# Fourteen projection units of each layer with a 512-column moving operand, and an evacuation in two steps

## What is computed

```python
u = rmsnorm(x, norm_mix[l])
proj = u @ w_in[l]                       # 1024 -> 5444 columns
q, k, v, iq, ik, iw, cB, cC, ch, g = jnp.split(proj, offsets, axis=-1)
y_attn = dsa_attention(q, k, v, iq, ik, iw) @ w_attn_out[l]      # top-64 keys by an index score
y_conv = (cB * short_conv(cC * ch, conv_w[l])) @ w_conv_out[l]
gates = jax.nn.sigmoid(g.reshape(B, T, N_BRANCH, D))
x = x + (gates[:, :, 0] * y_attn + gates[:, :, 1] * y_conv) @ w_mix_out[l]
u = rmsnorm(x, norm_mlp[l])
x = x + jnp.square(jax.nn.relu(u @ w_mlp_up[l])) @ w_mlp_down[l]
```

## Time and profile before

| | |
|---|---|
| median of three runs | 1065.11 us (1063.73 to 1068.13) |
| the profiled execution, its own time | 1065.51 us |
| its span, first to last instruction | 1063.7 us |
| busy: TensorE matmul, weight load | 1034.1 us (97%), 893.5 us (84%) |
| busy: VectorE, ScalarE, GpSimd | 708.1 us (67%), 535.5 us (50%), 69.6 us (7%) |
| granted TensorE clock, mean | 0.997 |

### The profile page before, as it was taken

How to read it: one execution, slowest core, us unless ns; L and a number is a source line. 1 busy time by engine, 2 the same in 40 slices (tenths; PEclk the granted TensorE clock), 3 DMA queues, 4 the chain that set the end, 5 groups by cost and what they waited for, 6 DMA issues and landing times.

```text
span 1063.7 us, 16558 instructions
## 1 busy us (share of the span) xinstructions
PE 1034.1 (97%) x6205; PEld 893.5 (84%) x6205; DVE 708.1 (67%) x1073; ACT 535.5 (50%) x687; POOL 69.6 (7%) x80
## 2 busy tenths in 40 slices
PE   8989989999999999999999999999999999999997
PEld 7865778888888899998788888888999987888886
DVE  6876766666667676768665656576776676655654
ACT  7546565444456544455634444375444645534443
POOL 1000000000000308000000000012170000000000
PEclk9999999999999999999999999999999999999999
DMA  9974335555555663248465563665622675566520
GB/s 296 215 236 153 119 114 203 198 172 192 174 183 164 202 189 120 77 172 292 133 209 189 178 212 109 222 200 159 199 95 85 220 236 172 185 197 199 161 95 39
DMA packets 130654, 185.16 MB, mean 174 GB/s; under 512 B 4361, under 2 KB 106399, under 8 KB 130591
## 3 DMA queue, kind: packets, MB, share of 16 engines
q1 hardware_dynamic: 130503, 184.25, 54.4%
q10 hardware_dynamic: 88, 0.04, 0.0%
HBM read 180.91 MB, written 1.56 MB: 172 GB/s over the span
## 4 chain that ended last, share of the span: by engine, by line
PE 89%; ACT 3%; DVE 3%; DMA 1%; SPq 1%; issue 1%; ACTq 0%; DVEq 0%
PE wide L553 17%; PE acc L516 9%; PE acc L517 9%; PE acc L518 9%; PE wide L554 9%; PE wide L516 7%; PE wide L517 7%; PE wide L518 7%; PE wide L536 3%; PE wide L529 3%; PE wide L530 3%; ACT whi L967 2%; SPq L430 1%; PE acc L686 1%; DVE wlo L1261 1%
## 5 line engine op out<-in xcount | busy, mean ns | idle before, releaser
L1261 DVE TENSOR_TENSOR wlo<-raw,whi 128x2048 fp32r<-128x2048 f32 (+1 forms) x178 | 386.8, 2180 | 155.5 <-ACT whi L967 154.3
L967 ACT ACTIVATE whi<-raw 128x2048 fp32r<-128x2048 f32 (+1 forms) x178 | 322.1, 1819 | 107.7 <-PE wide L518 43.9
L553 PE MATMUL wide<-uhl,whi 128*128 128x512 f32 x864 | 307.6, 399 | 4.5 <-DVE wlo L1261 4.5
L554 PE MATMUL wide<-uhl,wlo 128*128 128x256 f32 x864 | 242.4, 281 | 0.0
L553 PEld LDWEIGHTS wide<-uhl,whi 128*128 128x128 f32 x864 | 162.3, 188 | 44.9 <-DVE wlo L1261 5.8
L554 PEld LDWEIGHTS wide<-uhl,wlo 128*128 128x128 f32 x864 | 163.2, 189 | 1.4
L516 PE MATMUL acc<-whi,mhi 128*128 128x512 f32 x376 | 147.7, 393 | 1.9 <-DVE wlo L1261 1.7
L516 PE MATMUL wide<-uhl,whi 128*128 128x256 f32 x512 | 146.9, 287 | 1.1 <-DVE wlo L1346 1.0
L517 PE MATMUL acc<-wlo,mhi 128*128 128x512 f32 x376 | 146.8, 390 | 0.0
L518 PE MATMUL acc<-whi,mlo 128*128 128x512 f32 x376 | 146.6, 390 | 0.0
L517 PE MATMUL wide<-uhl,whi 128*128 128x256 f32 x512 | 144.9, 283 | 0.0
(11 more groups left out here) (248 smaller groups left out, 1212.4 us busy)
## 6 DMA issues: line engine op xcount, KB each, us to landing
raw<-in_w_in SPq DMA_DIRECT2D x49, 1024.0 KB, 5.4
raw<-in_w_mlp_up SPq DMA_DIRECT2D x32, 1024.0 KB, 5.8
raw<-in_w_mlp_down SPq DMA_DIRECT2D x32, 1024.0 KB, 4.9
raw<-in_w_gate SPq DMA_DIRECT2D x11, 1024.0 KB, 5.5
raw<-in_w_up SPq DMA_DIRECT2D x11, 1024.0 KB, 5.5
raw<-in_w_down SPq DMA_DIRECT2D x11, 1024.0 KB, 5.6
raw<-in_w_mix_out SPq DMA_DIRECT2D x8, 1024.0 KB, 5.3
raw<-in_w_out SPq DMA_DIRECT2D x4, 1024.0 KB, 10.9
```

What stands on the lines that cost most here:

```text
L553: pe.matmul(col[2 * n + c][:], whi_v(u)[:, f, cs], uhl[:, f, :], start=start, stop=False)
L554: return pe.matmul(col[2 * n + c][:, 0:T], wlo_v(u)[:, f, cs], uhl[:, f, 0:T], start=False, stop=stop)
L967: act.activation(whi[:, u.buf, 0:size], raw[:, u.slot, 0:size], ACT.Copy).then_inc(w_hi, 1)
L1261: dve.tensor_tensor(wlo[:, u.buf, 0:size], raw[:, u.slot, 0:size], whi[:, u.buf, 0:size].bitcast(F32), ALU.subtract).then_inc(w_lo, 1)
```

## The change

The units 8 to 21 of both layers go through `wide_features(u, j % 2)`: 32 matmuls, 16 of 512 and 16 of 256 columns, into both banks of the pair `wide[j % 2]`. A unit now shares its banks with the unit two before it, so TensorE waits from j = 10 on for the evacuation of unit j-2 (before: of unit j-4). The wait for the tokens of unit 7 comes at j = 9 and no longer at j = 10. The evacuation is in three instructions: ScalarE copies the low halves into the destination (it waits for the matmuls, in iteration j, behind the split and ahead of the copy of the probabilities), then VectorE, where L1570 stood, adds the high halves from the banks, waits for its own result (`link`), and multiplies by `rnb`.

```diff
@@ TensorE, the loop over a layer's units
-                    if j >= L_FIRST:
-                        pe.wait_ge(w_lo, u.upto())
-                    if j in (4, 6, 8, 10):
-                        pe.wait_ge(evac, A_TOKENS + L_TOKENS * l + j // 2 - 1)
-                    if j >= 12:
-                        pe.wait_ge(fevac, A_FEATURES + L_FEAT * l + j - 11)
+                    if j in (4, 6, 8, 9):
+                        pe.wait_ge(evac, A_TOKENS + L_TOKENS * l + (4 if j == 9 else j // 2 - 1))
+                    if j >= 10:
+                        pe.wait_ge(fevac, A_FEATURES + L_FEAT * l + j - 9)
...
                     else:
-                        col_features(u, col[j % 4], uhi, ulo)
+                        pe.wait_ge(w_lo, u.upto())
+                        wide_features(u, j % 2)
@@ ScalarE
                     elif j in (3, 5, 7):
                         evacuate_tokens(u, j, (qtok, ktok, vtok)[j // 2 - 1])
+                    elif j >= L_FIRST:
+                        act.wait_ge(used, u.upto())
+                        if j in (8, 10):
+                            act.wait_ge(qk_ps, 4 * (1 + l) + j - 6)
+                        act.activation(feature_dst(j), wide[j % 2][:, :, T:2 * T], ACT.Copy).then_inc(flow, 1)
@@ VectorE, feature_evac(j)
-                    dve.wait_ge(used, l_unit(l, j).upto())
...
-                    if j in (8, 10):
-                        dve.wait_ge(qk_ps, 4 * (1 + l) + j - 6)
-                    dve.tensor_tensor(dst, col[j % 4][:].rearrange("p (c t) -> p c t", c=2),
-                                      rnb[:].unsqueeze(1).broadcast_to([P, 2, T]), ALU.mult).then_inc(fevac, 1)
+                    dve.wait_ge(flow, L_FEAT * l + j - L_FIRST + 1)
+                    link(dve.tensor_tensor(dst, wide[j % 2][:, :, 0:T], dst, ALU.add))
+                    dve.tensor_tensor(dst, dst, rnb[:].unsqueeze(1).broadcast_to([P, 2, T]), ALU.mult).then_inc(fevac, 1)
```

More of the change, by code:

```diff
@@ L78 @@
 G_N = G_LAYER + LAYERS * LG_N
-LAYER_LINKS = 91
+LAYER_LINKS = 105
 L_FIRST = 8
@@ L266, in build @@
         fevac = sem("fevac")
+        flow = sem("flow")
         rn_ok = sem("rn_ok")
@@ L391, in mid, with feature_dst @@
             return buf[:, 2 * s:2 * s + 2, :]
+        def feature_dst(j):
+            return (cC, cH, cB)[(j - 8) // 2][:, 2 * (j % 2):2 * (j % 2) + 2, :] if j < 14 else \
+                big[:, 2 * (j - 14):2 * (j - 14) + 2, :]
         def t_bank(a, h):
@@ L1562, in feature_evac @@
                 def feature_evac(j):
-                    dst = (cC, cH, cB)[(j - 8) // 2][:, 2 * (j % 2):2 * (j % 2) + 2, :] if j < 14 else \
-                        big[:, 2 * (j - 14):2 * (j - 14) + 2, :]
-                    dve.wait_ge(used, l_unit(l, j).upto())
+                    dst = feature_dst(j)
                     if j == L_FIRST:
                         dve.wait_ge(rb_sb, 3 + l)
-                    if j in (8, 10):
-                        dve.wait_ge(qk_ps, 4 * (1 + l) + j - 6)
-                    dve.tensor_tensor(dst, col[j % 4][:].rearrange("p (c t) -> p c t", c=2),
-                                      rnb[:].unsqueeze(1).broadcast_to([P, 2, T]), ALU.mult).then_inc(fevac, 1)
+                    dve.wait_ge(flow, L_FEAT * l + j - L_FIRST + 1)
+                    link(dve.tensor_tensor(dst, wide[j % 2][:, :, 0:T], dst, ALU.add))
+                    dve.tensor_tensor(dst, dst, rnb[:].unsqueeze(1).broadcast_to([P, 2, T]), ALU.mult).then_inc(fevac, 1)
                 dve.tensor_copy(lg[:], gcol[:, bass.ds(l * LG_N + G_LAYER, LG_N)]).then_inc(lg_ok, 1)
```

## The result

The changed kernel takes 1084.87 us (median of four runs, 1083.03 to 1086.01); the ratio to the kernel before is 1.0154, with a 95% interval of 1.0129 to 1.0179. It is slower, as forecast, but by more: the forecast was 1078.0, and the median lies 0.9 us above the range of 1072 to 1084. On the 1065.11 us from which forecast and range were worked out, the ratio gives 1081.5 us, inside the range. The runs of one kernel lie up to 9 us apart (29 runs of the kernel before in a later comparison: 1063.14 to 1071.77, median 1068.48), and the slower ones show the lower granted clock of TensorE: a mean of 0.989 to 0.993 in the six slowest of the 29, of 0.993 to 0.997 in the eight fastest. In the changed kernel's trace the clock falls well under 1 at five places during matmuls, and four of them lie outside the changed stretches.

What follows compares the result with a forecast made beforehand. TensorE, busy 97% of the span, was taken as the bound, so each new wait counts in full. Matmul savings against evacuation waits lose 6.5 us a layer, 13.0 on 1065.51, less 0.4 for the median: 1078.0 us, range 1072 to 1084.

Steps and rivals of the forecast that it cites:

- the walk: Start times computed unit by unit from unit 8 to unit 23, each waiting for the evacuation two units before.
- Term 1: TensorE's matmuls, units 8 to 21: 5.63 us a unit instead of 5.76, saving 0.13 each, 3.6 over 28 units.
- Term 2: Units 8 to 13: evacuation lag grows from 5.03 to 6.26 us, so the stage loses 1.00 us.
- Term 3: Units 14 to 19: the add lengthens VectorE's and ScalarE's softmax loop by 2.92 us; unit 19 starts 6.1 us later.
- the old meeting: One softmax step a layer beside GpSimd's long multiplication, 2.57 us against a median of 0.33; the loop grew by 1.3.
- The bound: Meetings with GpSimd may not come back, 1075.5 us, or may cost another 1 us a layer, 1080.
- GpSimd is held up: Rival, chance 0.20: the new multiplication from SBUF delays GpSimd or softmax steps, 2 us a layer more, 1082.
- Term 4: Units 20 to 23: unit 23 waits 0.5 us for unit 21's evacuation; the layer loses 6.5 us.
- The sum: Both layers: 2 x 6.5 = 13.0 us on 1065.51, with the median 0.4 lower: 1078.0 us.
- The clock rival: Rival, chance 0.06: TensorE's new waits lower its clock in both layers' stages, some 10 us more, 1088.
- It fits: Rival, chance 0.08: evacuations finish in time, TensorE keeps its stride and gains 3.6 us, 1061.5.

Runs made afterwards that it cites:

- the reordered one: Changed kernel with VectorE's evacuation (add and multiplication) of unit j-1 moved ahead of its split of unit j+2: 1068.4 us, ratio 1.0009 to the kernel before.

## Why the prediction was right, and where its sizes were off

The mechanism was the one forecast: TensorE waits for the evacuation of the unit two before, first by its lag, then by VectorE's loop. As a difference from the kernel before, 13.0 us were forecast, with 7 to 19 as the range, and 16.4 measured. The starts follow the walk closely. Starts of units behind that of unit 8 (measured: the rows above less 375.40, before: the earlier trace rows less 372.14, as the first matmul of unit 8 shows 0.08 us early in both, at 375.32 and 372.06):

| | forecast | measured | before |
|---|---|---|---|
| unit 13 | 29.93 | 30.15 | |
| unit 15 | 44.44 | 44.95 | 41.60 |
| unit 19 | 76.09 | 77.07 | 69.91 |
| unit 23 | 100.56 | 101.87 | 94.01 |

- *Term 1, the matmuls.* The first pairs of unit 8 come every 0.347 us (376.45 to 379.92 for ten), so 5.55 us a unit and not 5.63, while later units show the 0.352 of the earlier trace rows. The saving is 0.13 to 0.2 us a unit. None of it could be seen in the changed kernel, but the reordered one shows it: unit 14 starts 1.26 us earlier than before. The sign and place were right. The 0.04 us a unit that the prediction worked out from the Trainium skill (TensorE: Matmul & The Clock Gate, "Wait — 56ns, not 53.3ns?") would have been too little; the measured spacings decide.
- *Term 2, the lag.* The evacuation of unit 8 was over 6.25 us behind its unit, as forecast, and that of unit 9, with the key selection, some 6.8 (forecast 6.66). Two things were too small: the step from VectorE's end to TensorE's start, 0.14 us (387.21 to 387.35) where I took 0.06, and the first pair of a unit that has waited, 0.45 us (387.35 to 387.80) where I took 0.35. From unit 11 to unit 13 they make the 0.2. The walk also passed over a wait: by its own terms unit 10 waits for unit 8's evacuation until 384.09 (372.14 + 5.63 + 6.32), 11.95 behind unit 8, and it was measured at 11.95; the prediction had it start at 383.40. So all four units wait, and not mostly every other one. At unit 13 this changes nothing, as the wait of unit 11 is the longer one.
- *Term 3, the loop.* Right in kind: without GpSimd's work, four turns take 30.48 us, which is the old 28.73 with 2.92 more and without the 1.2 of the old meeting (one old turn took 7.71 us, 420.63 to 428.34, where its neighbours took 6.52). The term that was mis-sized is GpSimd. The forecast carried the old meetings over (1.2 us in the loop); in the changed kernel the whole cost of GpSimd is 2.0 us of stage (101.95 less 99.93). The bound said that they might vanish or grow by 1 us a layer; they grew. The rival "GpSimd is held up", given 0.20, was thus a part of the truth: the new multiplication took 1.08 us once and 1.20 once a layer in place of 0.69. But it was VectorE that paid, not the copy of the probabilities behind GpSimd's end: all of TensorE's waits are for L1578. GpSimd's own steps took up to 2.6 us before as well. Of the 1.3 us between forecast and measurement in the table GpSimd is 0.8; the other 0.5 stand in the run without its work too (unit 23 at 99.85, forecast less the old meeting 99.36).
- *Term 4.* Unit 23 waited 0.67 us, forecast 0.5, and started 4.58 us behind unit 22 (472.69 to 477.27), forecast 4.33. The forecast had ScalarE's copy hidden there, and it isn't quite: the split behind it starts 0.87 us behind unit 22's start (473.56), and 0.72 before the change (463.03 against 462.31). The prediction also lacks ScalarE's table load of 1.28 us: before, it ran at 403.07, long ahead of the first head's exponentials; now it stands between unit 13's copy and them (412.11), and VectorE waits 1.23 us for them where it waits 1.05 at the later heads.
- *The sum.* 6.5 us a layer against 7.85: twice 1.35 short, 2.7 of the 6.9 us between forecast and median. Another 3.4 are the base, and that part is chance: 1065.11 was the median of three runs, and that of 29 later ones is 1068.5. The last 0.8 lie within the spread of the runs.
- *The clock rival,* 0.06. That the new waits would leave the clock alone, as the row at 100 to 104 us did, was wrong: it fell behind the wait before unit 15 in the first layer, and not in the second. Yet both stages took the same time, as TensorE was waiting for VectorE anyway. In other versions such a fall did cost: about 1.4 us behind the third head with the evacuation first and the banks given back at the add, and 1.4 and 1.2 us behind unit 19 in one layer each of the run without the copy (101.80 against 100.43) and of that with the banks given back at the add (101.37 against 100.22).
- *"It fits", 0.08.* Refuted for this order. With the other order TensorE keeps its stride through units 8 to 14, but a wait for the third head eats the gain. What decides is, as its sentence said, where the evacuation stands.

## What to carry to other kernels

Halving the number of buffers halves the slack of whoever gives them back. Look up when each buffer is given back, in the order of the engine that does it, before asking whether that engine has time: VectorE was idle for 30% of units 14 to 21 and still late. If the evacuation is short and the work ahead of it long, put it first; that was worth 8 us a layer here and cost no instruction. Where GpSimd and VectorE work side by side, look for VectorE's steps that end together with a long GpSimd instruction; cutting that one in four took 0.5 us off each layer's stage here.

## What the runs showed of the hardware

- A pair of VectorE's tensor_scalar, 0.68 us alone, ended 0.14 us behind a GpSimd instruction of 2.38 us and took 2.76; once that was cut into pieces of 0.72 to 1.18 us, the pair took 1.14. A tensor_scalar of two elements, 0.17 us alone, took 1.90 and ended with a GpSimd instruction of 2.40. GpSimd's 128x256 steps took 0.61 to 0.74 us alone and 2.55 to 2.67 where a split of VectorE, with both inputs in SBUF, ran at their start. The Trainium skill (SBUF — State Buffer, "Who interferes with whom") has this as an exclusive lock between VectorE and GpSimd, held for a whole instruction, and the rows agree.
- TensorE's wait of 1.86 us before unit 15 was followed by a clock of 0.61 in the first layer, and the same wait in the second by one of 1.00, in one execution with the same work on every engine. Windows of the changed kernel:

```profile
420.00:424.00 4.00, 3.65 (x13) 3.12 (x14) 2.68 (x10) 2.44 (x5) 3.61 (x6) 0.61 0.38 131
796.00:800.00 4.00, 3.58 (x20) 3.13 (x21) 2.75 (x10) 2.38 (x5) 3.61 (x6) 1.00 0.42 131
```

The columns are those of the earlier trace rows; the clock is the third from the end. Both stages took the same time all the same.
